# Inverse levels as 32x32 blocks with constant products between, fewer gate columns and a 48-row gate product in a two-layer hybrid trunk

## The reference

```python
mod = silu(c) @ mod_w[i] + mod_b[i]               # 6 x 2048 columns of a layer
h = rms_norm(x, g) * (1 + sc) + sh
# layer 0
log_f = log_sigmoid(f_logit + b_f); cum = cumsum(log_f)
logits = q @ k.T * scale + cum[q] - cum[k]        # causal, softmax, times v
# layer 1, per frame t and head
S_t = S_(t-1) diag(w_t) - (S_(t-1) kk_t)(kk_t * a_t)^T + v_t k_t^T
y_t = S_t r_t
```

## Time and profile before

| | us |
|---|---|
| median of 3 runs | 2939.6 |
| lowest, highest | 2933.57, 2946.09 |
| the profiled execution | 2940.58 |
| its span | 2938.5 |

### The profile page before, as it was taken

One profiled execution on the slowest core, in us unless ns is written; L12 is line 12 of the kernel. 1 busy time (PEld: TensorE's weight loads), 2 busy tenths in 40 slices (PEclk: granted clock), 3 DMA queues, 4 the chain that ended last, 5 costly groups with the idle time before them and its releaser, 6 DMA issues. The chain is left out here.

```text
span 2938.5 us, 57079 instructions
## 1 busy us (share of the span) xinstructions
PE 2768.2 (94%) x22010; PEld 2442.7 (83%) x22010; DVE 2094.1 (71%) x2726; ACT 1426.0 (49%) x1977; POOL 142.2 (5%) x160
## 2 busy tenths in 40 slices
PE   4599999899999999997999999998989999999998
PEld 3499998788888888885988788887878888888887
DVE  7877888888888876568865455554986666666665
ACT  2143334555555554446754333333456666664433
POOL 0000000000000000000000123120100000000000
PEclk8699999999999999998999999999989999999999
DMA  9968888778888768782655332223946566667875
GB/s 313 322 227 297 295 288 305 273 245 283 273 282 276 233 194 267 247 267 84 191 190 192 112 101 63 90 89 110 357 150 187 184 187 185 187 184 231 259 246 167
DMA packets 513063, 634.28 MB, mean 216 GB/s; under 512 B 27160, under 2 KB 451976, under 8 KB 512648
## 3 DMA queue, kind: packets, MB, share of 16 engines
q1 hardware_dynamic: 508864, 628.94, 65.7%
q10 hardware_dynamic: 4040, 3.07, 0.3%
HBM read 629.83 MB, written 2.10 MB: 215 GB/s over the span
## 5 line engine op out<-in xcount | busy, mean ns | idle before, releaser
L1290 DVE TENSOR_TENSOR wlo<-raw,whi 128x1024 fp32r<-128x1024 f32 x792 | 965.8, 1223 | 509.8 <-ACT whi L826 508.0
L826 ACT ACTIVATE whi<-raw 128x1024 fp32r<-128x1024 f32 x792 | 834.3, 1058 | 863.3 <-PE ps L2034 500.5
L2031 PE MATMUL ps<-xs,whi 128*128 128x512 f32 x3328 | 1173.9, 398 | 26.0 <-DVE xs L1716 15.0
L2034 PE MATMUL ps<-xs,wlo 128*128 128x256 f32 x3328 | 933.9, 281 | 0.0
L2031 PEld LDWEIGHTS ps<-xs,whi 128*128 128x128 f32 x3328 | 627.2, 188 | 178.3 <-issue 27.0
L2031 PE MATMUL ps<-act,whi 128*128 128x512 f32 x1920 | 676.9, 396 | 6.7 <-DVE wlo L1290 6.7
L2034 PEld LDWEIGHTS ps<-xs,wlo 128*128 128x128 f32 x3328 | 630.7, 190 | 0.0
L2034 PE MATMUL ps<-act,wlo 128*128 128x256 f32 x1920 | 539.1, 281 | 0.0
L2031 PEld LDWEIGHTS ps<-act,whi 128*128 128x128 f32 x1920 | 361.3, 188 | 90.0 <-DVE wlo L1290 8.1
L2034 PEld LDWEIGHTS ps<-act,wlo 128*128 128x128 f32 x1920 | 364.5, 190 | 0.0
L1312 DVE SCALAR_TENSOR_TENSOR macc<-raw,cact,macc 128x1024 f32<-128x1024 f32 (+1 forms) x266 | 324.5, 1220 | 12.5 <-DMA raw<-in_mod_w 6.5
(11 more groups left out here) (269 smaller groups left out, 3019.2 us busy)
## 6 DMA issues: line engine op xcount, KB each, us to landing
raw<-in_ffn_w_in SPq DMA_DIRECT2D x352, 512.0 KB, 4.3
raw<-in_mod_w SPq DMA_DIRECT2D x272, 384.0 KB, 4.6
raw<-in_mod_w SPq DMA_DIRECT2D x192, 512.0 KB, 5.8
raw<-in_ffn_w_out SPq DMA_DIRECT2D x176, 512.0 KB, 4.6
raw<-in_fox_w_in SPq DMA_DIRECT2D x96, 512.0 KB, 5.8
raw<-in_fox_w_out SPq DMA_DIRECT2D x32, 512.0 KB, 7.3
raw<-in_rwkv_w_r SPq DMA_DIRECT2D x32, 512.0 KB, 4.3
raw<-in_rwkv_w_k SPq DMA_DIRECT2D x32, 512.0 KB, 3.5
```

What stands on the lines that cost most here:

```text
L826: sc.activation(whi[:, half, :, :].rearrange("p k n -> p (k n)"), slots[slot], ACT.Copy).then_inc(w_hi, 1)
L1290: v.tensor_tensor(wlo[:, half, :, :].rearrange("p k n -> p (k n)"), slots[slot], whi[:, half, :, :].rearrange("p k n -> p (k n)").bitcast( ...
L2031: pe.matmul(ps[bank + m][:, :], whi[:, half, k, m * P:m * P + P], src[:, kt, :, :].rearrange("p u s -> p (u s)"), start=kt == 0, stop=Fals ...
L2034: last = pe.matmul(ps[bank + m][:, 0:S], wlo[:, half, k, m * P:m * P + P], src[:, kt, 0, :], start=False, stop=kt == n * PIECE_KT - 1, ski ...
```

## The change

- Levels 1 to 4: z and u are made for the two 32x32 diagonal blocks of each 64x64 matrix, four independent products (two heads, two blocks) in a row; level 5 makes only the 32x32 block that the mask copies.
- `keep_busy`: products of the identity with ones, 128x128, into a bank that nobody reads: 1 behind each z, 3 behind each u of levels 1 to 4, 12 and 3 in `chunk_head`.
- `chunk_head`: TensorE waits for the memsets (`pone`) behind `kk_norms` and no longer ahead of `loras`; ScalarE waits for `hw0` in place of `pone`.
- `gemv` makes tiles 46 to 63: two tiles a lap in laps 0 to 5, three in the last two.
- The gate's weights stand three times side by side, so its rows are 48; rows 0 to 15 then hold the rounded part and rows 32 to 47 the rest (`nparts`), `gsel` picks both, and `scores` has one selection product for two.
- The attention lap's `adaln_sum` moves from the lap's end into the next lap's first slab, two columns behind each of the first three weight pieces; that of the last lap goes between the first pieces of the output projection.

```diff
+    def chunk_tiles(i):
+        return (46 + 2 * i, 2) if not isinstance(i, int) or i < 6 else (58 + 3 * (i - 6), 3)
...
+        nparts = take(r, "nparts", [GATE_ROWS, S])
+        nsel = take(r, "nsel", [GATE_ROWS, 2, S], F32R)
...
-            sc.dma_start(bf[:, :], a["fox_b_f"].rearrange("o h -> h o")).then_inc(fox_in, 16)
+            for n in range(3):
+                sc.dma_start(bf[HEADS * n:HEADS * n + HEADS, :], a["fox_b_f"].rearrange("o h -> h o")).then_inc(fox_in, 16)
...
-            sc.wait_ge(fox_in, 48)
-            sc.activation(wfh[:, :, :], wf[:, :, :], ACT.Copy).then_inc(*fg_a.inc("hi"))
+            sc.wait_ge(fox_in, 80)
+            sc.activation(wfh[:, :, :].rearrange("p k (c n) -> p k c n", c=3),
+                          wf[:, :, :].unsqueeze(2).broadcast_to([P, KT, 3, HEADS]), ACT.Copy).then_inc(*fg_a.inc("hi"))
...
-                sc.wait_ge(*pr_v.at("pone"))
+                sc.wait_ge(*pr_v.at("hw0"))
...
+                v.wait_ge(*fg_v.at("nlo"))
+                v.tensor_copy(nparts[0:HEADS, :], neghi[0:HEADS, :].bitcast(F32)).then_inc(*fg_v.inc("nparts"))
...
-                    for u, src in enumerate((neghi[:, :].bitcast(F32), neglo[:, :])):
-                        v.tensor_scalar(nsel[:, h, u, :], src, con[0:HEADS, ds(a_ * 2 + (K_ID + h), 1)], None,
-                                        ALU.mult).then_inc(*at_v.inc(f"sel{h}{u}"))
+                    v.tensor_scalar(nsel[:, h, :], nparts[:, :], gsel[:, ds(a_ * 2 + h, 1)], None,
+                                    ALU.mult).then_inc(*at_v.inc(f"sel{h}"))
...
-                    hooks[3] = lambda: adaln_out(ph_fox, i - 2)
+                    hooks[7] = lambda: adaln_out(ph_fox, i - 2)
...
-                        for u in range(2):
-                            last = pe.matmul(dst, oner[:, :], nsel[:, h, u, 0:n], start=False, stop=u == 1,
-                                             skip_group_check=True)
+                        last = pe.matmul(dst, oner[:, :], nsel[:, h, 0:n], start=False, stop=True,
+                                         skip_group_check=True)
...
-            with pe.Fori(1, 8) as i:
+            def fox_lap(i, first):
                 scores(i - 1)
-                slab(ph_fox, i - 1, 0, 4, 0, xs)
+                slab(ph_fox, i - 1, 0, 4, 0, xs,
+                     between=None if first else lambda q: adaln_sum(ph_fox, i - 2, 0, q, 3) if q < 3 else None)
                 probs(i - 1)
                 slab(ph_fox, i - 1, 4, 4, 1, xs)
                 values(i - 1)
                 slab(ph_fox, i - 1, 8, 4, 2, xs, tokens=True)
-                adaln_sum(ph_fox, i - 1)
+            fox_lap(1, True)
+            with pe.Fori(2, 8) as i:
+                fox_lap(i, False)
             scores(7)
-            paired_slab(ph_fox_out, 0, 0, 0, act, only=(0,))
+            paired_slab(ph_fox_out, 0, 0, 0, act, only=(0,), between=lambda q: adaln_sum(ph_fox, 6, 0, 0, 2))
             probs(7)
-            paired_slab(ph_fox_out, 0, 0, 0, act, only=(1,))
+            paired_slab(ph_fox_out, 0, 0, 0, act, only=(1,), between=lambda q: adaln_sum(ph_fox, 6, 0, 1, 2))
...
-                        last = pe.matmul(ps[7][32 * g:32 * g + 32, 0:384], cst[:, kt, :],
-                                         slots[ph_chunk.raw(k)][:, 384 * e:384 * e + 384], start=b == 0, stop=b == 3,
+                        n = chunk_tiles(i)[1] * P
+                        last = pe.matmul(ps[7][32 * g:32 * g + 32, 0:n], cst[:, kt, :],
+                                         slots[ph_chunk.raw(k)][:, n * e:n * e + n], start=b == 0, stop=b == 3,
...
+            def keep_busy(n, bank=7):
+                for _ in range(n):
+                    pe.matmul(ps[bank][:, 0:P], ident, ones, start=True, stop=True, skip_group_check=True)
             def chunk_head(i, q):
-                pe.wait_ge(*pr_v.at("pone"))
                 loras(i)
                 lora_gate(i, False)
                 kk_norms(i)
+                pe.wait_ge(*pr_v.at("pone"))
+                keep_busy(12)
                 kk_spread(i)
+                keep_busy(3)
                 bonuses(i)
...
-                                last_ = small_mm(ps[p][h, c * HD:(c + 1) * HD], lnm[h, p, c, :],
-                                                 ut[q][h, p, c, 0, :])
+                                if n == LEVELS - 1:
+                                    lower = slice(h.start + HB, h.stop)
+                                    last_ = small_mm(ps[p][h.start:h.start + HB, c * HD + HB:(c + 1) * HD],
+                                                     lnm[lower, p, c, 0:HB], ut[q][lower, p, c, 0, HB:HD])
+                                    continue
+                                for b in range(2):
+                                    r_, at_ = slice(h.start + b * HB, h.start + b * HB + HB), slice(b * HB, b * HB + HB)
+                                    last_ = small_mm(ps[p][r_, c * HD + b * HB:c * HD + b * HB + HB], lnm[r_, p, c, at_],
+                                                     ut[q][r_, p, c, 0, at_])
                         last_.then_inc(*c_.inc(f"z{n}p{p}"))
+                    keep_busy(1, 2)
...
-                                last_ = small_mm(ps[2 + p][h, c * P:c * P + HD], ut[q][h, p, c, 1, :], zsb[h, p, c, :])
-                                if n < LEVELS - 1:
-                                    last_ = small_mm(ps[2 + p][h, c * P + HD:(c + 1) * P], zsb[h, p, c, :],
-                                                     ut[q][h, p, c, 1, :])
+                                if n == LEVELS - 1:
+                                    upper = slice(h.start, h.start + HB)
+                                    last_ = small_mm(ps[2 + p][upper, c * P + HB:c * P + HD], ut[q][upper, p, c, 1, 0:HB],
+                                                     zsb[upper, p, c, HB:HD])
+                            if n == LEVELS - 1:
+                                continue
+                            for u in range(2):
+                                for h in heads:
+                                    for b in range(2):
+                                        r_, at_ = slice(h.start + b * HB, h.start + b * HB + HB), slice(b * HB, b * HB + HB)
+                                        dst = ps[2 + p][r_, c * P + u * HD + b * HB:c * P + u * HD + b * HB + HB]
+                                        full, part = ut[q][r_, p, c, 1, at_], zsb[r_, p, c, at_]
+                                        last_ = small_mm(dst, *((part, full) if u else (full, part)))
                         last_.then_inc(*c_.inc(f"u{n}p{p}"))
+                    if n < LEVELS - 1:
+                        keep_busy(3, 0)
```

More of the change, by code:

```diff
@@ L47 @@
 HEADS = 16
+GATE_ROWS = 48
 LORA = 96
@@ L50 @@
 CH = S // HD
+HB = HD // 2
 NR, NH = 4, 4
@@ L709, in gemv_pieces @@
                         sp.wait_ge(gemv_used, i * (KT // 4) + ((k - NR) // 2 + 1))
-                    sp.dma_start(slots[slot][:, 0:768].rearrange("p (k n) -> p k n", k=2),
-                                 mod_w[1][:, 2 * k:2 * k + 2, ds(i * 384 + 40 * P, 384)]).then_inc(raw_in[slot], 16)
+                    tile, n = chunk_tiles(i)
+                    sp.dma_start(slots[slot][:, 0:2 * n * P].rearrange("p (k n) -> p k n", k=2),
+                                 mod_w[1][:, 2 * k:2 * k + 2, ds(tile * P, n * P)]).then_inc(raw_in[slot], 16)
             sp.wait_ge(w_used, ph_rkv[2].weight(3, 7))
@@ L717, in _ @@
                 gemv_pieces(i)
-            with sp.Fori(2, ph_chunk.iters - 1) as i:
+            with sp.Fori(2, ph_chunk.iters - 2) as i:
                 sp.wait_ge(*hd_pe.at("lg", i))
@@ L721, in _ @@
                 gemv_pieces(i)
+            sp.wait_ge(*hd_pe.at("lg", ph_chunk.iters - 2))
+            lora_second(ph_chunk.iters - 1)
+            gemv_pieces(ph_chunk.iters - 2)
             gemv_pieces(ph_chunk.iters - 1)
@@ L1485, in gate_weights @@
             def gate_weights():
-                v.tensor_copy(oner[:, :], ones[0:HEADS, :]).then_inc(*fg_v.inc("one"))
+                v.tensor_copy(oner[:, :], ones[0:GATE_ROWS, :]).then_inc(*fg_v.inc("one"))
+                v.tensor_tensor(gsel[:, :], ident[0:GATE_ROWS, 0:HEADS], ident[0:GATE_ROWS, 32:32 + HEADS],
+                                ALU.add).then_inc(*fg_v.inc("sel"))
                 v.wait_ge(*fg_a.at("hi"))
-                v.tensor_tensor(wfl[:, :, :], wf[:, :, :], wfh[:, :, :].bitcast(F32), ALU.subtract).then_inc(
-                    *fg_v.inc("lo"))
+                v.tensor_tensor(wfl[:, :, :].rearrange("p k (c n) -> p k c n", c=3),
+                                wf[:, :, :].unsqueeze(2).broadcast_to([P, KT, 3, HEADS]),
+                                wfh[:, :, :].bitcast(F32).rearrange("p k (c n) -> p k c n", c=3),
+                                ALU.subtract).then_inc(*fg_v.inc("lo"))
             w = 0
@@ L1518, in gate_first @@
                 v.wait_ge(*fg_pe.at("z"))
```

(10 more changed lines are left out.)

40 lines of the change are left out of this document (21 added, 19 removed).

## The result

The changed kernel takes **2976.9 us** (median of 4 runs, 2974.0 to 2982.3) where the kernel before took 2936.6 (4 runs, 2929.9 to 2946.1). The ratio is 1.0138, 95% interval 1.0110 to 1.0165: 40 us slower, and above the high end of the predicted range. Its profiled execution took 2982.3 us, 41.7 more than that of before.

What follows compares the result with a forecast made beforehand. TensorE's instruction stream (94% busy) was taken as the bound, up to a VectorE and ScalarE chain before solve(0). Gains 19.6 + 3.5 + 6.1 - 1.4 + 8 - 1 = 34.8 off 2940.6 gave 2906 us, range 2890 to 2940.

Steps and rivals of the forecast that it cites:

- part 1: Chunk laps, inverse levels 1 to 4: 32x32 records at 8 ns each save 4.8 us a lap.
- rival A: 32x32 records come slower than 8 ns, 5.6 us per extra ns; 2928 us at 12 ns; chance 0.14.
- rival C: TensorE's clock falls in the chunk laps; 6.8 us at half clock a lap gives 2933, 10.2 gives 2947; chance 0.13.
- Part 2: Constant products behind z and u in the chunk laps lose 2.9 us a lap.
- X: VectorE and ScalarE chain, last level-4 copy to solve(0), 6.99 us; savings before it count, those behind it become idle time.
- Part 3: Chunk laps' mod_w product, 256 columns for 384 in laps 0 to 5: 0.7 us a lap won.
- Part 4: Head of the chunk stage: earlier start by 1.7 us and constants holding the clock win 3.5 us, bounds 1.5 to 4.5.
- Part 5: Attention laps: one selection product for two wins 6.1 us, splitting moved sums costs 1.4, the clock's recovery wins 8.
- Part 6: Gate's start: 48 rows for 16 add a copy and wider weight operations, 1 us lost, bounds 0 and 2.

Runs made afterwards that it cites:

- e5: Changed kernel with 64x64 products at levels 1 to 5, each issued as two with half the moving columns, no constant products in the laps; 3158.7 us.
- e7: e1 plus z of levels 1 to 4 in 32x32 blocks and the single block at level 5, u of levels 1 to 4 whole; 2916.4 us.
- e3: Changed kernel with 64x64 products at all levels again, constant products in the laps kept; 2954.4 us, ratio 1.0059 to the kernel before.
- e1: Changed kernel with 64x64 products at all levels again and no constant products in the laps; 2915.6 us, ratio 0.9918 to the kernel before.
- e2: Changed kernel without the constant products in the laps, 32x32 blocks kept; 2973.4 us, ratio 1.0121 to the kernel before.
- e4: Changed kernel with 64 moving columns for 32 in each block product, same number of instructions; 2973.3 us, ratio 1.0108 to the kernel before.
- e10: e7 with six constant products added just ahead of solve(0), where TensorE waits; 2920.0 us, ratio 0.9952 to the kernel before.

## Why the prediction was wrong

**The step that failed** is in part 1: "That instructions can be handed over fast enough is in the same place: eight weight loads". Those eight loads are a burst of instructions that were already there. The 32x32 records did take 8.4 ns, the end that I chose, but only up to the end of the packet: where the next packet was late, TensorE halted, 20 times for 28.9 us from start to start, at multiples of 256 instructions. I had noted against rival A that "those are a burst of eight, where u needs 128 in a row", priced that doubt as a slower pace per record, and not as halts. The row that bounded it was on the page of before, unread: q8's 118 packets, 7 or 8 in each lap. At 955 matmuls and 955 loads a lap, one packet is some 250 instructions; the change asks for 256 in one u of level 4, in 1.1 us.

**The second step** is rival C. The clock did fall, for 10 to 17 us in a full lap, at or above the 10.2 that I had priced at 2947. Its chance of 0.13 was too small, and it came on top of the halts, not instead of them: e5, and e7's lap from 1721.8, show the fall without any halt. What makes it fall stays open.

**Part 2** was mis-sized: constants 2.9 us a lap, measured 4.1 (e3). 1.1 of that is behind X: from the last level-4 copy to solve(0) it is 7.87 us in e3 and 6.77 in e1, because level 4's triple and level 5's single one delay the level-5 copies. I had said that the triple lies behind the last product that X needs, and forgot the chain that starts there.

**What held.** X is the bound: 7.02 us in the undisturbed laps of the changed kernel (6.9 to 7.0 said), with 0.7 to 1.1 us of idle time ahead of solve(0) where I had said 1.6. Part 3: 0.9 for 0.7. Part 4: the head is 1.5 us shorter and its start no longer waits 1.67 us, 3.2 together for 3.5; but from the last score to the head's first product it is 1203.9 us for 1203.4, so the 1.67 does not show in the sum of this execution. Part 5: the clock holds in every attention lap, and the start-to-last-score distance falls from 301.3 us to 290.5, 10.8 for a sum of 12.7. Its selection products gave less. TensorE's timeline of the changed kernel, to be held against the earlier trace rows:

```profile
198.60 0.33 PE L2165 MATMUL ps<-nsel,oner 48*128 48x128 f32 x1
198.85 0.70 PE L2163 MATMUL ps<-kf,qf 128*128 128x256 f32 x2
199.48 0.39 PE L2165 MATMUL ps<-nsel,oner 48*128 48x256 f32 x1
199.80 0.49 PE L2163 MATMUL ps<-kf,qf 128*128 128x128 f32 x2
```

One product stands 0.25 and 0.32 us ahead of the next where two stood 0.36 and 0.43: 0.11 less each, 0.44 a lap for 0.76. I had charged the removed one by its start-to-start distance inside the pair; the one that stays takes more than its half. Part 6: the first score starts at 158.6 for 156.9, 1.7 us for 1.0.

**The books**, in the profiled executions: 11.3 us won ahead of the laps (15.2 predicted for parts 4 to 6), 53.6 lost in them (19.6 predicted as a gain), 0.6 won elsewhere: 41.7 lost. Against e3, which has the same constants, the blocks cost 25.3 us: 28.9 us of halts, up to 44 of the clock (89 us more at half, if all of it were TensorE's), less the 38 that quicker products save, and the rest I take to lie in waits that were there anyway. That split is worked out from single executions, not measured: what each halt and each clock stretch costs by itself stays open.

## What to carry to other kernels

Small products have a price in instructions, not only in columns: before splitting one product into two, count instructions per microsecond in the densest stretch and hold them against the packets of the instruction queue in the trace. Here 256 instructions came every 3.4 us at best. Code in a short loop needed no packets here, as in the attention laps; no run tried a loop for the chunk laps. A burst in the trace shows what the engine can do, not what it can be fed. Where a change bundles parts, the parts that hold may be carried off alone: this change without its blocks and the constants in its laps is 0.8% faster than the kernel before by four runs, of which the profiles place about 0.4% in what was edited.

## What the runs showed of the hardware

- Four 32x32 quadrants in turn take an fp32 record each 8.4 ns from start to start (32 in 0.27 us), with 64 moving columns 14 ns, and 64x64 weights about 30 ns whether 64 or 32 columns move. The Trainium skill's floor of about 25 ns (TensorE: Matmul & The Clock Gate, "Wait — 56ns, not 53.3ns?") does not hold across quadrants here.
- TensorE's instructions arrive in packets of 16,384 bytes, 256 instructions. All 89 halts that no semaphore ended lie at a multiple of 256 instructions from each other; a starved stream goes on 2.15 to 2.9 us after a packet starts, in 83 of them, and the shortest distance between the starts of two packets is 3.4 us in the changed kernel and 3.3 in any (e2). In a loop of attention laps no packet came for 170 us.
- The clock fell to 0.50 with TensorE nearly always busy (e5, 0.67 over a lap of 81.8 us at 80.7 busy), and stayed at 1.00 through 15 halts of up to 1.8 us from start to start (e4). Constants in an idle place did not keep it up (e10).
